# FFN up-projection: two plainly computed feature pairs in place of three, token combinations ahead of weight sums on GpSimd, splits in the order of use

## What is computed

```python
h2 = _rmsnorm(x, g_pre_ffn) * (1 + sc2) + sh2
up = _dwconv_rows(jnp.einsum('bld,df->blf', h2, w_up), conv_w, conv_b, grid)
ug, uv = jnp.split(up, 2, axis=-1)
f = jnp.einsum('blf,fd->bld', jax.nn.gelu(ug) * uv, w_down)
x = x + gt2 * _rmsnorm(f, g_post_ffn)
```

## Time and profile before

| what | us |
|---|---|
| median of 3 runs | 1883.65 |
| the 3 runs | 1883.33 to 1884.7 |
| profiled execution, its own time | 1886.68 |
| span in its trace, first to last instruction | 1884.9 |
| mean granted TensorE clock, share of full | 0.992 |

### The profile page before, as it was taken

One profiled execution on the slowest core, in us unless ns is written; L12 is line 12 of the kernel. 1 busy time (PEld: TensorE's weight loads), 2 busy tenths in 40 slices (PEclk: granted clock), 3 DMA queues, 4 the chain that ended last, 5 costly groups with the idle time before them and its releaser, 6 DMA issues.

```text
span 1884.9 us, 27369 instructions
## 1 busy us (share of the span) xinstructions
PE 1839.7 (98%) x10922; PEld 1721.2 (91%) x10922; DVE 1076.2 (57%) x2271; ACT 712.5 (38%) x1220; POOL 225.4 (12%) x240
## 2 busy tenths in 40 slices
PE   7999999999999999999999998899999999999997
PEld 2999999999999999999998898899999999888886
DVE  2663545555555553345454566777777777757563
ACT  3633322244243233253243443444444444444432
POOL 2000000000000010011000026222222221002011
PEclk9999999999999999999999999899999999999999
DMA  9123323313323344157232221223332234868682
GB/s 348 34 86 93 79 65 93 102 62 122 106 71 100 105 121 145 49 202 238 91 91 90 101 93 51 83 95 107 112 103 96 97 100 140 307 225 291 220 285 92
DMA packets 202562, 239.96 MB, mean 127 GB/s; under 512 B 9944, under 2 KB 162548, under 8 KB 202436
## 3 DMA queue, kind: packets, MB, share of 16 engines
q1 hardware_dynamic: 185204, 174.88, 29.5%
q0 software_dynamic: 12736, 45.56, 7.1%
q10 hardware_dynamic: 4496, 17.77, 2.3%
HBM read 180.50 MB, written 57.68 MB: 126 GB/s over the span
## 4 chain that ended last, share of the span: by engine, by line
PE 89%; DVE 4%; ACT 2%; POOL 2%; DMA 1%; issue 1%; SPq 0%; ACTq 0%; DVEq 0%; POOLq 0%
PE ps L1205 21%; PE ps L1233 13%; PE ps L888 13%; PE ps L890 13%; PE ps L889 13%; PE ps L1143 5%; PE ps L1024 2%; PE ps L1027 2%; PE ps L1026 1%; POOL T_full L579 1%; PE ps L930 1%; PE ps L1003 1%; PE ps L915 1%; DMA adaw<-in_w_ada_dram 1%; DVE H_lo L1794 1%
## 5 line engine op out<-in xcount | busy, mean ns | idle before, releaser
L888 PE MATMUL ps<-H_hi,ring_hi 128*128 128x384 f32 x1416 | 493.0, 348 | 6.2 <-DVE H_lo L1794 4.3
L890 PE MATMUL ps<-H_hi,ring_lo 128*128 128x384 f32 x1416 | 476.3, 336 | 0.0
L889 PE MATMUL ps<-H_lo,ring_hi 128*128 128x384 f32 x1416 | 476.0, 336 | 0.0
L888 PEld LDWEIGHTS ps<-H_hi,ring_hi 128*128 128x128 f32 x1416 | 267.9, 189 | 10.1 <-DVE H_lo L1794 5.3
L889 PEld LDWEIGHTS ps<-H_lo,ring_hi 128*128 128x128 f32 x1416 | 268.0, 189 | 1.1
L890 PEld LDWEIGHTS ps<-H_hi,ring_lo 128*128 128x128 f32 x1416 | 267.3, 189 | 0.0
L1942 DVE SCALAR_TENSOR_TENSOR Cst<-Cst,Et,ps 128x257 f32<-128x257 f32 x64 | 30.9, 484 | 222.1 <-PE ps L1027 222.1
L1205 PE MATMUL ps<-T_hi,up_hi 128*128 128x288 f32 x608 | 131.2, 298 | 12.1 <-DVE T_lo L1794 12.1
L1205 PE MATMUL ps<-T_hi,up_lo 128*128 128x288 f32 x608 | 131.1, 297 | 0.0
L1205 PE MATMUL ps<-T_lo,up_hi 128*128 128x288 f32 x608 | 131.0, 297 | 0.0
L1794 DVE TENSOR_TENSOR down_lo<-down_raw,down_hi 128x1024 fp32r<-128x1024 f32 x66 | 80.7, 1223 | 76.2 <-ACT f_hi L1699 76.2
(11 more groups left out here) (278 smaller groups left out, 3305.4 us busy)
## 6 DMA issues: line engine op xcount, KB each, us to landing
down_raw<-in_w_down_dram SPq DMA_DIRECT2D x66, 512.0 KB, 3.9
raw<-in_w_in_dram SPq DMA_DIRECT2D x44, 512.0 KB, 3.9
up_raw<-in_w_up_dram SPq DMA_DIRECT2D x38, 512.0 KB, 5.2
raw<-in_w_ada_dram SPq DMA_DIRECT2D x32, 512.0 KB, 4.8
f_raw<-z_gate SPq DMA_DIRECT2D x66, 192.0 KB, 3.7
v_raw<-z_value SPq DMA_DIRECT2D x66, 192.0 KB, 4.1
z_gate<-mid_g SPq DMA_DIRECT2D x38, 288.0 KB, 4.2
z_value<-mid_v SPq DMA_DIRECT2D x38, 288.0 KB, 4.6
```

Source lines behind the costliest of these rows:

```text
L888: pe.matmul(out, whi, xhi, start=first, stop=False)
L889: pe.matmul(out, whi, xlo, start=False, stop=False)
L890: return pe.matmul(out, wlo, xhi, start=False, stop=last)
```

## The change

- `PLAIN` goes from 3 to 2: pair 2 moves to the seven-product scheme, so 20 pairs are computed by it.
- GpSimd makes the token combinations of k = 0, 1 and 2 one behind the other, and only then the weight sums of pair s = 0.
- VectorE and ScalarE: `up_lo`/`up_hi` 0 and 1 of the first combined pair come directly behind plain pair 0, ahead of the combinations of k = 3; the splits of k = 0 and 3 follow; then plain pair 1. Within plain pair 1, the split of k = 1 stands between its gate and its value half; the split of k = 2 comes behind the pair, then weights 2 to 5.
- The places of the split weights in the ring (`up_at`) and five waits follow the new order.

```diff
-PLAIN = 3
+PLAIN = 2
...
-    up_at = [RING0 + 4096 * n for n in (0, 3, 1, 4, 2, 5)] + [LD0 + 8192]
+    up_at = [RING0 + 4096 * n for n in (1, 4, 2, 5, 0, 3)] + [LD0 + 8192]
...
-            sp.wait_ge(lo_ready, S_FF + 2 * PLAIN - 1)
+            sp.wait_ge(lo_ready, S_FF + 2 * PLAIN)
...
-                        pool.wait_ge(lo_ready, S_FF + 2 * PLAIN)
+                        pool.wait_ge(lo_ready, S_FF + 2 * PLAIN - 1)
...
             for n, k in enumerate(range(KD // 2 - 1)):
                 quarter_tiles(pool, pool_sums, k, 8 * n)
-                if n == 0:
-                    for j in range(4):
-                        weight_sum(0, j)
-            for s in range(1, NP):
+            for s in range(NP):
                 for j in range(4):
                     weight_sum(s, j)
...
                 elif i in (0, 1):
-                    act.wait_ge(done1, 3 * KD + NB * (PLAIN - 1))
+                    act.wait_ge(done1, 3 * KD + NB)
...
                     if f == 1 and half:
                         gate_copy(gtb2, 1, 3)
+                        quarter_split(1)
...
             gate_copy(gtb2, 0, 2)
-            plain_up(1, [[4], [5]])
-            for k in (KD // 2 - 1, 0):
-                quarter_split(k)
             up_hi_split(0, 0)
             up_hi_split(0, 1)
-            plain_up(2, [[], []])
-            for i in (2, 3):
-                up_hi_split(0, i)
-            for k in range(1, KD // 2 - 1):
-                quarter_split(k)
-            for i in (4, 5):
+            quarter_split(0)
+            quarter_split(3)
+            plain_up(1, [[], []])
+            quarter_split(2)
+            for i in range(2, 6):
                 up_hi_split(0, i)
...
                     for j in splits[half]:
                         ff_lo(j)
+                    if f == 1 and half:
+                        quarter_split(1, 2)
...
             plain_up(0, [[2], [3]])
-            quarter_tiles(dve, dve_sums, KD // 2 - 1, 0)
-            plain_up(1, [[4], [5]])
-            for n, k in enumerate((KD // 2 - 1, 0)):
-                quarter_split(k, n)
             next_weights(-1, 0)
             next_weights(-1, 1)
-            plain_up(2, [[], []])
-            for i in (2, 3):
-                next_weights(-1, i)
-            for k in range(1, KD // 2 - 1):
-                quarter_split(k, k + 1)
-            for i in (4, 5):
+            quarter_tiles(dve, dve_sums, KD // 2 - 1, 0)
+            quarter_split(0, 0)
+            quarter_split(3, 1)
+            plain_up(1, [[], []])
+            quarter_split(2, 3)
+            for i in range(2, 6):
                 next_weights(-1, i)
```

More of the change, by code:

```diff
@@ L2109, in _, with quarter_split @@
             norm_split(NB * KD, tsc2, 2, NB - 1)
+            def quarter_split(k, n):
+                dve.wait_ge(quarter_hi, n + 1)
+                for name in quarters:
+                    ins = sub_hi(T_lo[name][:, k, :], T_full[name][:, k, :], T_hi[name][:, k, :])
+                ins.then_inc(quarter_lo, 1)
             def plain_up(f, splits):
@@ L2151, in plain_up @@
                 assert n[0] == 8 * (f + 1)
[L2153 to L2158, removed]
             def up_lo_split(s, i):
```

## The result

| | before | after |
|---|---|---|
| median of 5 runs | 1883.65 us | 1892.53 us |
| range of the runs | 1883.14 to 1884.7 | 1891.43 to 1893.94 |
| ratio, with 95% interval | 1 | 1.0047 (1.0033 to 1.0062) |
| span of the profiled run | 1884.9 us | 1890.7 us |

A forecast was written before the change was run, and what follows sets the result against it. TensorE, busy 98% of the span, bounds the kernel, except for a wait ahead of the first quarter product. X 13.3 us earlier plus 22.4 for one more combined pair gives +9.1 on 1883.65: 1892.8 us, range 1882.5 to 1896.5.

The forecast's parts named there:

- the 18 instructions: VectorE's 2 up_lo, 8 combinations of k = 3 and 8 T_lo between plain pairs 0 and 1; forecast to end at 1149.7.
- wait ahead of product 0: TensorE idle 16.8 us until the gate taps of plain pair 1 end on VectorE; product 0 starts at 1156.0.
- Xs: Time from the stage's start to the first product that uses a quarter; 82.2 us before the change.
- X: Time at which product 2 of the first combined pair starts on TensorE; 1182.87 before, forecast 1169.6.
- The formula of the end: Span changes by (X - 1182.87) + 22.38 us, as the same work plus one combined pair follows X.
- The turn of 1.87 us for all 18 instructions: VectorE and working GpSimd do one instruction each per 1.87 us; 17 turns take 31.8 us, ending at 1149.7.
- Rival 1: VectorE and GpSimd hardly disturb each other; X = 1151, time 1874.2 us; chance 0.12.
- Rival 2: VectorE keeps the port while instructions are queued, only 8 combinations take turns; X = 1162, 1885.2 us; chance 0.18.
- Rival 3: Whole VectorE and GpSimd instructions exclude each other, 2.15 us a turn; X = 1174.4, 1897.6 us; chance 0.07.
- The second wait: TensorE idle 4.8 us ahead of product 2, after products 0 and 1 end at 1164.8, until up_lo 2.
- GpSimd's new order: GpSimd makes k = 1 and 2 directly behind k = 0; k = 2 ready at about 1143.5, not 1177.6.

The follow-up runs named there:

- second comparison: The changed kernel itself, unaltered, timed again beside the kernel before on the same chip: 1895.40 us, ratio 1.0068.
- e5: Changed kernel with each of GpSimd's 16 steps for k = 1 and 2 replaced by two memsets that write but read nothing: 1873.65 us, ratio 0.9954.
- e6: Changed kernel with GpSimd's order alone undone, weight sums of the first pair again ahead of k = 1 and 2: 1892.71 us, ratio 1.0056.
- e1: Kernel before, three plain pairs, with only GpSimd's order changed to k = 0, 1 and 2 in a row, then weight sums: 1872.98 us, ratio 0.9941.
- e7: Kernel before with GpSimd's new order, both T_hi and VectorE's k = 1 split ahead of pair 2, k = 2 between its halves: 1869.17 us, ratio 0.9931.
- e2: Kernel before with GpSimd's new order and the splits of k = 1 and 2 between the halves of plain pair 2: 1873.38 us, ratio 0.9943.

## Why the prediction was right

**Measured 1892.53, forecast 1892.8, and for the reasons given.** The agreement to 0.3 us is luck, since the second comparison gave a loss of 12.9 us where the forecast was 9.1 and the first measured 8.9. The agreement of the steps is not luck. The steps, each from the stage's start (1100.69 before, 1097.49 after):

| step | forecast us | trace us |
|---|---|---|
| plain pair 1 ends on TensorE | 38.5 | 38.7 |
| the 18 instructions end on VectorE | 49.0 | 48.9 |
| product 0 starts | 55.3 | 55.2 |
| wait ahead of product 0 | 16.8 | 16.4 |
| value taps of pair 1 end | 65.6 | 65.4 |
| wait ahead of product 2 | 4.8 | 5.4 |
| first quarter product, Xs | 68.9 | 68.8 |
| X to the end against before | +22.4 | +22.4 |

- *The formula of the end* held in all ten traces to about 1 us, once the low clock behind X is counted. Here the low clock behind X lasted 3.6 us, where the forecast had taken the 4.5 us of before.
- *The turn of 1.87 us for all 18 instructions* was the one uncertain term, and it held: 1.87 for a combination, 1.84 for a `T_lo` (14.73 us for eight), 2.92 for the two `up_lo` of which the first came into a turn that had begun. It had been taken from four `T_lo` in one place of the trace before. e5 shows its cause, reads by both engines.
- *Rival 1*, engines that hardly disturb each other, is refuted by 1.87 against 0.76. Its price was about right: 9.5 us less than before by the forecast, 8.9 less in e5, where the reads are gone.
- *Rival 2*, VectorE keeps the port, is refuted for rows of `T_lo`, which took turns. What it rested on is real, though: the first weight sum behind X was overtaken again (below).
- *Rival 3*, whole instructions exclude each other, 2.15 us a turn, is refuted by the same rows.
- *The second wait* was 0.6 us longer than forecast. Products 0 and 1 took 8.3 us and not 8.8, since the clock returned earlier behind the first wait.
- *That GpSimd's new order buys k = 2 at 1143* was right, and e6 shows that it bought nothing with two plain pairs. The prediction said what the changed list costs, and did not say that the order would be worth 11 us with three pairs (e1), and 13 us with the splits moved to suit it (e7).

What stays open: why GpSimd gets its turn in the middle of a row of `T_lo` but seems to be overtaken by `up_lo` behind a pause. No run was made for it.

## What to carry to other kernels

Work that is moved to an idle engine is not free where both engines read SBUF at the same time: look in the trace for a place where the two already run side by side, and price the moved list at that rate, not at the rate it had alone. Before cover is removed from a critical path (here 25 us of plain matmuls for a gain of 2.6 us), first move the hidden work and see whether the cover is still needed. And an order that puts each result just ahead of its use has to be written for the pair of engines that hand it over; in e2 the late half on ScalarE cost 2.9 us on VectorE.

## What the hardware showed

- Two engines taking turns are cheaper than one behind the other: a GpSimd step of 1.43 us and a VectorE one of 0.67 to 0.79 us took 1.87 to 1.91 us together, not 2.2. The Trainium skill (SBUF — State Buffer, "Who interferes with whom") has the loser block for the whole instruction; here 0.2 to 0.3 us of each pair overlaps.
- GpSimd's first sum behind X took 2.77 to 2.80 us in nine of the ten traces, where such a sum alone takes 1.29, and looks overtaken: in the changed kernel VectorE's row of four `up_lo` took 2.49 us, its own pace, and the sum ended 1.15 us behind it. A pause alone does not slow it, since in the trace of before a sum behind 18.99 us of rest took 1.29. In e7 the same sum took 1.59 and the four `up_lo` 3.59. In the changed kernel:

```profile
1168.14 2.79 POOL L853 TENSOR_TENSOR up_s<-up_raw 128x512 f32<-128x512 f32 x1 [20.67 <-DVE up_lo L1788]
1171.01 1.29 POOL L853 TENSOR_TENSOR up_raw<-up_raw 128x512 f32<-128x512 f32 x1
```

- Behind a wait of TensorE of 3.2 us the granted clock stood at 0.50 in e1, from 1170.8 to 1176.0; in e7, with a wait of 0.5 us at the same place, at 1.00. The wait of 1.92 us ahead of the stage was followed by the low clock in six traces and not in four. So a wait that is nearly closed can still cost clock as well as time, in e1 1.9 us from X to the end against e7:

```profile
1170.80:1176.00 5.20, 5.20 (x22) 5.20 (x23) 3.58 (x6) 0.00 (x0) 3.85 (x2) 0.50 0.41 120
```
